# Eight of a network's modulation tiles are worked on at other places of the same instruction streams

## The reference, cut to what matters

```python
def modulate(h, shift, scale):
    return h * (1 + scale[:, None, :]) + shift[:, None, :]
...
cs = jax.nn.silu(c)
for l in range(DEPTH):
    if l == N_A_LAYERS:
        kv_mod = cs @ kv_mod_w + kv_mod_b
        kv = shared_kv(x, kv_mod[:, :D], kv_mod[:, D:], kv_norm, w_kv)
    mod = cs @ mod_w[l] + mod_b[l]          # 1024 x 6144
    ...
    x = x + g_m[:, None, :] * mix
    h = modulate(rmsnorm(x, norm_ffn[l]), sh_f, sc_f)
    x = x + g_f[:, None, :] * swiglu(h, ffn_w_gate[l], ffn_w_up[l], ffn_w_down[l])
```

## Time and profile before

| | before |
|---|---|
| three runs | 2248.55, 2250.91, 2251.79 us |
| median | 2250.91 us |
| span of the profiled execution | 2244.5 us |
| PE busy | 2200.6 us (98%) |
| DVE busy | 1544.8 us (69%) |
| ACT busy | 1168.8 us (52%) |
| HBM read | 422.87 MB |

### The profile page before, as it was taken

The page is one execution under the profiler, slowest core; times in us unless marked ns, Lnnn a source line. Parts: engine busy times, 40 slices in busy tenths (PEclk is TensorE's granted clock), DMA queues, the critical chain, the costliest instruction groups (busy, mean ns, idle before and its releaser), DMA issues.

```text
span 2244.5 us, 40835 instructions
## 1 busy us (share of the span) xinstructions
PE 2200.6 (98%) x17072; PEld 2140.3 (95%) x17072; DVE 1544.8 (69%) x2549; ACT 1168.8 (52%) x1950; POOL 19.9 (1%) x27
## 2 busy tenths in 40 slices
PE   7999999999999999999999999999999999999999
PEld 6889998999999999999999999999999999999998
DVE  6858996776669588755655766486879655657663
ACT  3635444554444567445644644444766456546443
POOL 0000000000000000000000100000000000001000
PEclk9999999999999999999999999999999999999999
DMA  9958996456655555454444555556654544454563
GB/s 366 334 177 336 364 383 234 135 189 223 193 172 175 173 189 159 143 160 134 127 155 153 167 178 163 176 169 184 195 170 145 177 130 132 150 179 161 186 179 114
DMA packets 123189, 428.18 MB, mean 191 GB/s; under 512 B 14528, under 2 KB 18816, under 8 KB 122368
## 3 DMA queue, kind: packets, MB, share of 16 engines
q1 hardware_dynamic: 123008, 425.58, 57.9%
HBM read 422.87 MB, written 2.66 MB: 190 GB/s over the span
## 4 chain that ended last, share of the span: by engine, by line
PE 84%; DVE 8%; DMA 4%; ACT 2%; issue 1%; SPq 0%; ACTq 0%; DVEq 0%
PE stream L507 25%; PE stream L509 24%; PE stream L508 24%; PE stream L513 4%; DVE w_lo L405 2%; DMA raw<-in_ffn_up 2%; PE side L660 2%; DVE mod_raw L1422 1%; PE side L667 1%; ACT w_hi L925 1%; DMA raw<-in_ffn_down 1%; DMA mod_raw<-in_mod_w 1%; DMA x_res<-in_x 1%; PE side L589 1%; PE side L801 0%
## 5 line engine op out<-in xcount | busy, mean ns | idle before, releaser
L507 PE MATMUL stream<-h_hi,w_hi 128*128 128x272 f32 (+1 forms) x3344 | 966.2, 289 | 8.5 <-DVE conv_out L1614 5.0
L509 PE MATMUL stream<-h_hi,w_lo 128*128 128x272 f32 (+1 forms) x3344 | 955.8, 286 | 0.0
L508 PE MATMUL stream<-h_lo,w_hi 128*128 128x272 f32 (+1 forms) x3344 | 953.4, 285 | 0.0
L405 DVE TENSOR_TENSOR w_lo<-raw,w_hi 128x1024 fp32r<-128x1024 f32 (+1 forms) x642 | 770.5, 1206 | 169.3 <-ACT w_hi L925 167.8
L925 ACT CAST w_hi<-raw 128x1024 fp32r<-128x1024 f32 (+1 forms) x642 | 654.2, 1035 | 271.1 <-DMA raw<-in_ffn_down 98.6
L507 PEld LDWEIGHTS stream<-h_hi,w_hi 128*128 128x128 f32 x3344 | 631.6, 189 | 14.7 <-issue 8.2
L509 PEld LDWEIGHTS stream<-h_hi,w_lo 128*128 128x128 f32 x3344 | 631.6, 189 | 0.0
L508 PEld LDWEIGHTS stream<-h_lo,w_hi 128*128 128x128 f32 x3344 | 630.8, 189 | 0.4
L507 PE MATMUL stream<-f_hi,w_hi 128*128 128x256 f32 (+1 forms) x704 | 199.5, 283 | 1.5 <-DVE x_res L1481 1.4
L509 PE MATMUL stream<-f_hi,w_lo 128*128 128x256 f32 (+1 forms) x704 | 198.9, 283 | 0.0
L508 PE MATMUL stream<-f_lo,w_hi 128*128 128x256 f32 (+1 forms) x704 | 198.4, 282 | 0.0
(11 more groups left out here) (345 smaller groups left out, 3018.9 us busy)
## 6 DMA issues: line engine op xcount, KB each, us to landing
raw<-in_ffn_up SPq DMA_DIRECT2D x176, 512.0 KB, 4.3
mod_raw<-in_mod_w SPq DMA_DIRECT2D x96, 512.0 KB, 5.5
raw<-in_ffn_down SPq DMA_DIRECT2D x64, 512.0 KB, 4.2
raw<-in_a_cx SPq DMA_DIRECT2D x32, 512.0 KB, 4.2
raw<-in_up_a SPq DMA_DIRECT2D x32, 512.0 KB, 3.5
raw<-in_up_b SPq DMA_DIRECT2D x32, 512.0 KB, 3.5
raw<-in_b_kq SPq DMA_DIRECT2D x32, 512.0 KB, 3.5
raw<-in_up_c SPq DMA_DIRECT2D x32, 512.0 KB, 3.5
```

Source lines behind the costliest of these rows:

```text
L405: eng.tensor_tensor(w_lo[:, x.slot, 0:x.kb * P], raw[:, x.slot, 0:x.kb * P], w_hi[:, x.slot, 0:x.kb * P].bitcast(F32), ALU.subtract).then_ ...
L507: pe.matmul(ps, w_hi[:, x.slot, W], rhs[0][:, k, off:off + n], start=first, stop=False)
L508: pe.matmul(ps, w_hi[:, x.slot, W], rhs[1][:, k, off:off + n], start=False, stop=False)
L509: return pe.matmul(ps, w_lo[:, x.slot, W], rhs[0][:, k, off:off + n], start=False, stop=last)
```

## The change

Four modulation tiles fewer are spread over `ffn_up0` (36 instead of 40) and four fewer over the first twenty chunks of `ffn_down0` (16 instead of 20). Four are put into `ffn_down0`'s last chunk through the new field `late`, and four into `kv_v`, one per chunk. Tiles stay in their order, so each of the later ones is computed by a place further on in the list than before.

```diff
     def __init__(self, name, kind, n, rhs="H", parts=(8,), off=0, T=TOK, l=0, t0=0, norm=None, lead=1, mods=0,
-                 raw=0, raw_of=None, raw_rhs=None, plain=False, quiet=0):
+                 raw=0, raw_of=None, raw_rhs=None, plain=False, quiet=0, late=0):
...
-        self.plain, self.quiet = plain, quiet
+        self.plain, self.quiet, self.late = plain, quiet, late
...
-          Phase("ffn_up0", "glu", 44, lead=4, mods=40, quiet=8, raw=4, raw_of="ffn0", raw_rhs="RA", **seq),
-          Phase("ffn_down0", "resid", 8, "F", (8, 8, 6), norm="kv", mods=20, **seq),
+          Phase("ffn_up0", "glu", 44, lead=4, mods=36, quiet=8, raw=4, raw_of="ffn0", raw_rhs="RA", **seq),
+          Phase("ffn_down0", "resid", 8, "F", (8, 8, 6), norm="kv", mods=16, late=4, **seq),
           Phase("kv_k", "act", 4, lead=4, raw=4, raw_of="kv", raw_rhs="HX", plain=True, **seq),
-          Phase("kv_v", "vtok", 4, raw=4, raw_of="kv", raw_rhs="HX", plain=True, **seq),
+          Phase("kv_v", "vtok", 4, mods=4, raw=4, raw_of="kv", raw_rhs="HX", plain=True, **seq),
...
     for p in ph:
+        p.mods_at[-1] += p.late
         p.mod_tiles = []
```

## The result

| | before | after |
|---|---|---|
| median | 2248.55 us | 2241.66 us |
| runs | 9, 2245.09 to 2254.34 | 9, 2240.76 to 2244.64 |
| ratio, 95% interval | | 0.9973, 0.9964 to 0.9981 |
| profiled execution, its own time | not given | 2241.51 us |
| span of it | 2244.5 us | 2239.6 us |

By the ratio the change makes the kernel 0.27% faster, 6.1 us (4.3 to 8.1 us by its interval); the two medians are 6.9 us apart. So of the 6.4 us that I had taken for what lies around the span, 1.9 us were that, and 4.5 us were the distance of the median of three runs from the one execution that I read.

The account below looks back on a forecast made before the run. It took PE as fullest, with DMA and DVE nearly full, and transfers as making DVE late. Span 2244.5 - 2.29 + 0.6 = 2242.8 us, plus 6.4 us, gave 2249.2 us; range 2246.0 to 2252.0 us.

Parts of the forecast that it names:

- the 6.4 us: Whole kernel: difference between the profiled execution's span and the median of the runs, added to the forecast span.
- -2.29 us: `ffn_up0` and `ffn_down0`: saving from closing two PE gaps, 0.74 and 1.55 us; bounds 0 and -2.77 us.
- the lateness comes from the transfers: `ffn_up0` and `ffn_down0`: transfers make DVE late; taking tiles out cuts demand per chunk from 388 to 368 GB/s.
- The bandwidth rule: HBM reads: about 358 GB/s per core would bind `ffn_up0`, each tile taken out saving 1.46 us; the prediction doubted it.
- Rival (a): Transfers set the stage's length: eight tiles give back 1.42 us each, 11.4 us together; 2240.1 us, chance 0.06.
- The gaps: PE waits at 275.93 us for DVE's `conv_out` (0.74 us) and 323.49 us for `x_res` (1.55 us); both forecast gone.
- the bound of 2.77 us: Largest saving in the stretch, if two small PE gaps at the border to `ffn_down0`, 0.48 us, go as well.
- The late tiles: Four tiles behind the last sums: cost 0, covered by DVE's 5.49 us wait for `rstd`, 0.7 us left.
- `kv_v`: Four tiles there delay `q`'s second load and the first transposes: +0.6 us, bounds 0 and 2.0 us.
- (b): `ffn_up0` and `ffn_down0`: DVE's lateness is inherited from early constant loads, both gaps stay; 2251.5 us, chance 0.15.
- (c): Tiles behind the sums outlast the `rstd` wait, so PE waits for `kv_k`'s first bank; 2252.6 us, chance 0.04.
- (d): The wait at `kv_v`'s first transposes grows over 3 us and PE's clock falls; 2252.3 us, chance 0.05.

Follow-up runs that it names:

- e1: The kernel before, unchanged, run and profiled once more; 2247.97 us, ratio 1.0005.
- e9: The kernel before, unchanged, one more profiled execution; 2250.69 us.
- e10: The kernel before, unchanged, another profiled execution; 2248.15 us.
- e11: Before with eight instead of four idle PE matmuls ahead of `ffn_up0`; 2249.61 us, ratio 0.9999.
- e2: Before with 36 tiles in `ffn_up0` and four in `kv_v`, but 20 kept in `ffn_down0` and none late; 2242.1 us, ratio 0.998.
- e4: Before, loading only half the columns of the 60 tiles in `ffn_up0` and `ffn_down0`, DVE still working on whole tiles; 2241.02 us, ratio 0.9974.
- e7: After with eight tiles instead of four behind the last sums and none in `kv_v`; 2246.62 us, ratio 0.9993 against before.
- e8: After with eight instead of four idle PE matmuls ahead of `ffn_up0`; 2241.45 us, ratio 0.9972 against before.
- e12: After with eight idle matmuls ahead of `ffn_up0` and `kv_v`'s four tiles moved into `q`; 2244.37 us, ratio 0.9985 against before.
- e13: Before with a fifth buffer in the ring of modulation tiles from tile 48 on, nothing else; 2240.59 us, ratio 0.9965.
- e15: After with the loads of `kv_v`'s four tiles issued behind `kv_v`'s weights, ahead of `q`'s loads; 2240.8 us, ratio 0.9965 against before.
- e6: Before with whole loads, but DVE summing only half the columns of the 60 tiles in `ffn_up0` and `ffn_down0`; 2242.48 us, ratio 0.9979.
- e5: Before with `ffn_up0`'s 40 tiles spread one per chunk over 40 chunks instead of 36; 2244.29 us, ratio 0.9983.
- e14: After with `ffn_up0`'s 36 tiles packed into 32 chunks, so four chunks have two; 2243.34 us, ratio 0.9976 against before.
- e3: Before with 16 tiles plus four late in `ffn_down0`, `ffn_up0` and `kv_v` left as before; 2244.76 us, ratio 0.9987.

## Why the prediction was wrong, and where it was right

**What failed first: one execution was read as all of them.** The sum took 2.29 us of gaps from one profile and put the saving there. The stretch of the profiled before was 174.19 us; the other four profiled executions (e1, e9, e10, e11) had 176.84, 178.21, 176.44 and 176.21 us. After, e2, e4, e7, e8, e12, e13 and e15 all lie between 171.16 and 171.22 us. The gain in the stretch is thus 3.0 to 7.0 us, 5.2 us in the mean of the five. The term "-2.29 us" was right for the execution it was read from (3.0 us measured) and half of the usual one. The timed runs shown had said so: three runs, 4.1 to 7.3 us above the profiled span. I put this down to "this execution's span and the median of the runs" and carried it over unchanged, a step with no row behind it. With 1.9 us around the span and the rest as stalls of the ordinary execution that the change could close too, the forecast would have been 2242.8 + 1.9 = 2244.7 us. Beside this the starting point was high by luck of the draw: the three runs shown have a median of 2250.91 us, the nine of the result 2248.55 us. The forecast missed by 7.5 us: 2.4 us are this, and 5.2 us that the medians fell by 6.9 us where I had 1.7 us.

**What failed second: the cause.** I wrote that "the lateness comes from the transfers", and set the demand of 388 GB/s against 369 and 381 GB/s moved. But what a full window moved is what it was given to move. e13 moved 397 and 400 GB/s with the same tiles. What held DVE up was the wait of SP for a ring buffer, with the weight loads queued behind it; DVE's lateness and the loads' lateness feed each other. I had seen that wait in the code before the prediction, and the sum did not use it. By it, a small relief anywhere in the loop should end or shorten the stalls: bytes (e4), DVE's work (e6), a buffer (e13) and tiles (after) left 0 to 0.4 us of them, and spacing alone (e5) 2.2 us.

**The bandwidth rule.** In e13 the core read 397 GB/s over 108 us and 400 GB/s over 32 us. The Trainium skill, "DMA: Bandwidth & Descriptors", section Bandwidth, says that for transfers between HBM and SBUF a limit of about 358 GB/s per core binds; by that rule the stretch would have been as long as its transfers and e13 impossible. The same section of the Trainium skill also measures 425 GB/s for one core and gives about 358 GB/s as a core's part when both cores of a pair are streaming, which I had left out. This kernel runs on one core, and its 397 GB/s agrees with the second reading and not with the first. The measurement decides. Rival (a), which was that rule as a mechanism, gave 2240.1 us. The measured time is nearer to that than to my forecast, and still the mechanism is not it: e4 took away some 16 MB, half of 60 tiles, and saved no more in the stretch (171.21 us) than e13, which took away nothing. 171.2 us is PE's own pace, and nothing more is to be had there.

**Part by part.** The gaps: gone, both, and so are the small ones at the border to `ffn_down0` (the bound of 2.77 us, 3.0 us measured in this pair of executions). The late tiles cost 0: right, with 2.58 us of DVE's wait for `rstd` left where I had reckoned with 0.7 us at the worst. `kv_v`: forecast +0.6 us with a wait of 1.2 to 1.9 us, measured 1.16 us in after, 1.12 in e2, 1.31 in e8 and 1.27 in e14, against 0.79 to 1.01 us in those without tiles there: +0.2 to +0.4 us. The mechanism, a tile's load ahead of `q`'s second, is right: e15 takes just that away and the wait goes to 0.74 us. `kv_k` starts 5.5 us earlier in the two profiles, of which 2.5 us are chance.

**The rivals.** (b), gaps that stay, did not happen; e3 shows that it would have been true at 272 and 276 us without the `ffn_up0` part. (c) does not happen with four tiles; e7 has it with eight. There the last tile ends 13.4 us behind `kv_k`'s start; in before `rstd` was used first at 364.3 us, 8.7 us behind it. So the tile is 4.7 us late. The reckoning of (c) gives 4.7 - 0.6 = 4.1 us of wait for that, and PE stands 4.64 us. What the reckoning leaves out is the clock behind the wait, 1.5 us. (d) did not happen in after: the wait in `kv_v` was 1.16 us and the clock 1.00. Its second half, a fall of the clock behind a long wait there, is what e7 shows.

**How much of it is clock.** The 95 timed runs of before beside e1 to e15 can be sorted by their mean clock. The median span is 2244.0 us in the 31 with 1.000, 2246.2 us in the 40 with 0.999, and 2248.7 us in the 24 with 0.998. After's nine have 2239.6 us in the five with 1.000 and 2241.8 us in the four with 0.999, and none has 0.998. So at equal clock the two kernels are 4.4 us apart, which is near the 5.2 us of the stretch less what `kv_v` costs. The rest of the difference of the medians goes with the clock: the middle run of before has lost some of it, that of after none. In e9 one such loss, 1.7 us, came behind a gap that the change takes away.

**What stays open.** In some executions the clock falls behind a gap (e9) or near 160 us (0.81 to 0.83 in the first profile, e9, e10 and e11), and in others of the same kernel it doesn't (e1). Why the wait near 160 us varies, why eight fillers did not hold the clock in e11, and why the same loop loses 3 us in one execution and 7 us in another, stays open. All kernels, after too, also have a long wait of ACT for a weight that ends between 210 and 222 us, of 4.0 us in e14 to 7.0 us in e11. In after it follows a 1 MB load of constants issued at 202.6 us; that this load causes it is not shown. After and e13 make it up without a gap on PE.

## What to carry to other kernels

When a stretch looks bound by DMA, read the waits of the issuing queue before trusting GB/s: if loads wait for a ring buffer that is freed by an engine which itself waits for loads, one more buffer (e13, 0.9965 alone) may be worth as much as moving work. Before a gain is summed from a profile, hold the profiled execution's own time against the median: where they differ, the ordinary execution may have stalls, or lose clock, where this profile doesn't show it; here it had longer gaps in the same places. And work put behind an engine's last task before a long wait is free only as far as that wait reaches: the 5.5 us here covered four tiles of 1.2 us, and not eight.

## What the runs showed of the hardware

- One core read 397 GB/s over 108 us and 400 GB/s over 32 us, nearly all of it in 512 KB loads (e13); 385 GB/s over 108 us in after.
- A queue that stands leaves the DMA engines empty only some us later: in e1 SP issued nothing from 268.9 to 274.73 us, and the share was 0.94, 0.47 and 0.16 in the three windows of 2 us from 270 us on.
- After a wait of 1.77 us the granted clock was 0.66 over the next 5 us in e9; after one of 2.27 us in e1 it stayed at 1.00. The length of the wait alone did not decide it.
- Behind PE's wait near 160 us, in the fourteen profiles with the usual filler, the clock fell in all six with a wait of 2.69 to 3.47 us and in none of the five with 1.53 to 1.97 us. Of the other three it fell behind 2.08 us (e3) and 2.19 us (e15) and not behind 2.25 us (after).
- Behind a wait of 4.64 us in e7 the granted clock was 0.65 over the next 4.2 us.
